# Five norms' running sums: tail tiles added on VectorE, fewer one-column sums on TensorE, root's table loaded earlier on ScalarE

## The reference

```python
def rmsnorm(x, g):
    return x * lax.rsqrt(jnp.mean(x * x, axis=-1, keepdims=True) + eps) * g
def _layer_norm(x, g, b):
    mu = jnp.mean(x, axis=-1, keepdims=True)
    var = jnp.mean(jnp.square(x - mu), axis=-1, keepdims=True)
    return (x - mu) * lax.rsqrt(var + LN_EPS) * g + b
# block 1
h = h + y @ w_out                                   # stage "out"
h = h + swiglu(rmsnorm(h, g_ffn), ...)              # "gu0", "down0"
h = rmsnorm(h, g_final)
# block 2, layer 0 and 1
x = _layer_norm(ALPHA * x + attention(x), ...)      # "out1", "out2"
x = _layer_norm(ALPHA * x + conv_ffn(x), ...)       # "gu1", "down1"; "gu2", "down2"
```

## Time and profile before

| | us |
|---|---|
| median of three runs | 1835.89 (1835.01 to 1836.67) |
| the profiled execution | 1835.84 |
| its span, first to last instruction | 1834.0 |
| TensorE busy | 1794.6 (98%) |
| GpSimd busy | 1034.7 (56%) |
| ScalarE busy | 783.4 (43%) |
| VectorE busy | 732.1 (40%) |

### The profile page before, as it was taken

The page is one execution under the profiler, slowest core; times in us unless marked ns, Lnnn a source line. Parts: engine busy times, 40 slices in busy tenths (PEclk is TensorE's granted clock), DMA queues, the critical chain, the costliest instruction groups (busy, mean ns, idle before and its releaser), DMA issues.

```text
span 1834.0 us, 26913 instructions
## 1 busy us (share of the span) xinstructions
PE 1794.6 (98%) x8816; PEld 1493.1 (81%) x8816; DVE 732.1 (40%) x1348; ACT 783.4 (43%) x1620; POOL 1034.7 (56%) x927
## 2 busy tenths in 40 slices
PE   8999999999999999999999999989999999999997
PEld 6879888888887888788888888878887888888886
DVE  7954000001125556453333322456765533333224
ACT  5434322332235556464444422545564644444221
POOL 6856665565562333466666654556554566656651
PEclk9999999999999999999999999999999999999999
DMA  5302333323334554323333232333332233332332
GB/s 150 92 23 82 104 102 98 96 77 109 88 86 113 133 127 114 97 66 109 92 102 91 84 106 86 81 81 87 91 79 57 78 103 100 94 99 82 103 90 96
DMA packets 327250, 171.92 MB, mean 94 GB/s; under 512 B 43458, under 2 KB 316948, under 8 KB 327188
## 3 DMA queue, kind: packets, MB, share of 16 engines
q1 hardware_dynamic: 327172, 171.12, 33.5%
q10 hardware_dynamic: 16, 0.00, 0.0%
HBM read 152.15 MB, written 2.10 MB: 84 GB/s over the span
## 4 chain that ended last, share of the span: by engine, by line
PE 83%; DVE 6%; ACT 4%; issue 2%; DMA 2%; SPq 1%; POOL 1%; ACTq 0%; DVEq 0%; POOLq 0%
PE bank L951 23%; PE bank L953 23%; PE bank L952 23%; PE attended L951 2%; PE attended L952 2%; PE attended L953 2%; DVE small L2324 1%; DMA raw<-in_a_w_in 1%; ACT pmap L1757 1%; PE turned L1348 1%; PE bank L1054 1%; PE bank L1042 1%; DVE PTL L2328 1%; ACT PTH L1762 1%; PE score L1332 0%
## 5 line engine op out<-in xcount | busy, mean ns | idle before, releaser
L720 POOL TENSOR_TENSOR WL<-raw,WH 128x512 fp32r<-128x512 f32 (+3 forms) x656 | 778.7, 1209 | 587.6 <-ACT WH L1514 586.9
L951 PE MATMUL bank<-XL,WH 128*128 128x512 f32 x1456 | 579.5, 398 | 7.1 <-DVE XL L2097 3.2
L953 PE MATMUL bank<-XH,WL 128*128 128x512 f32 x1456 | 567.9, 390 | 0.0
L952 PE MATMUL bank<-XH,WH 128*128 128x512 f32 x1456 | 567.7, 390 | 0.0
L1514 ACT ACTIVATE WH<-raw 128x512 fp32r<-128x512 f32 (+3 forms) x656 | 338.4, 566 | 306.3 <-PE bank L953 181.1
L951 PEld LDWEIGHTS bank<-XL,WH 128*128 128x128 f32 x1456 | 275.0, 189 | 62.3 <-DVE XL L2097 4.2
L953 PEld LDWEIGHTS bank<-XH,WL 128*128 128x128 f32 x1456 | 274.6, 189 | 58.2
L952 PEld LDWEIGHTS bank<-XH,WH 128*128 128x128 f32 x1456 | 275.1, 189 | 51.3
L951 PE MATMUL bank<-HL,WH 128*128 128x512 f32 (+1 forms) x528 | 200.6, 380 | 0.0
L952 PE MATMUL bank<-HH,WH 128*128 128x512 f32 (+1 forms) x528 | 200.3, 379 | 0.0
L953 PE MATMUL bank<-HH,WL 128*128 128x512 f32 (+1 forms) x528 | 200.3, 379 | 0.0
(11 more groups left out here) (322 smaller groups left out, 2474.4 us busy)
## 6 DMA issues: line engine op xcount, KB each, us to landing
raw<-in_ffn_w_in SPq DMA_DIRECT2D x88, 512.0 KB, 3.8
raw<-in_w_gate SPq DMA_DIRECT2D x22, 512.0 KB, 3.9
raw<-in_w_up SPq DMA_DIRECT2D x22, 512.0 KB, 3.8
raw<-in_ffn_w_out SPq DMA_DIRECT2D x28, 384.0 KB, 3.4
raw<-in_ffn_w_out SPq DMA_DIRECT2D x28, 320.0 KB, 3.2
raw<-in_a_w_in SPq DMA_DIRECT2D x16, 512.0 KB, 4.2
raw<-in_kv_w SPq DMA_DIRECT2D x32, 256.0 KB, 3.2
raw<-in_w_in SPq DMA_DIRECT2D x12, 512.0 KB, 3.9
```

The lines of the kernel that those rows point to most:

```text
L720: pool.tensor_tensor(wl, x, wh, ALU.subtract).then_inc(w_lo, 1)
L951: pe.matmul(out_, wh, xl, start=start, stop=False)
L952: pe.matmul(out_, wh, xh, start=False, stop=False)
L953: return pe.matmul(out_, wl, xh, start=False, stop=stop)
```

## The change

- **VectorE.** Behind `tail_out` of each half, new adds (`add_tail`) put each tail tile (layer norms only) and its squares into the running sums, 256 tokens at a time. Half 0: right behind each tail tile's residual add, values first and then the squares. Half 1: the values behind both residual adds, the squares behind pair 3. Behind out1 and out2 the sums stay in the PSUM banks until the last tail tile. The last add of squares raises the new counter `sum_full`.
- **TensorE.** `full_sums` takes the place of `whole_sums` and `half_stats` in the first five norms: 2 sums per half (RMS) or 4 (layer norm), behind a wait for `sum_full`. In half 0 it stands behind 5 of the 8 k of the first tail item (`SUMS_AT`), in the next stage behind k = 4; `half_widen` of half 1 moves from k = 5 to k = 6. In half 0 three k and one stand between sums and widening, where before it were four and one.
- **ScalarE.** `warm(ACT.Sqrt)` moves from behind the stage's last weight copy to the middle of the copies (out stages) or ahead of them (down stages), in all six places. The loop of `highs("out")` is written out.

```diff
+SUMS_AT = 5
@@ stage (out stages); the same in down
-                half_item(name, DT - 2, 0, hi, lo, 0, DT, 1, 0, 3)
-                whole_sums(m, 0)
-                half_item(name, DT - 2, 0, hi, lo, 0, DT, 1, 3, 4)
-                half_stats(m, 0)
-                half_item(name, DT - 2, 0, hi, lo, 0, DT, 1, 4).then_inc(item_done, 1)
+                half_item(name, DT - 2, 0, hi, lo, 0, DT, 1, 0, SUMS_AT)
+                full_sums(m, 0)
+                half_item(name, DT - 2, 0, hi, lo, 0, DT, 1, SUMS_AT).then_inc(item_done, 1)
@@ stage_in_halves
-                        if h == 0 and k == 2:
-                            whole_sums(m, 1)
-                        if h == 0 and k == 3:
-                            half_stats(m, 1)
-                        if h == 0 and k == 5:
+                        if h == 0 and k == 4:
+                            full_sums(m, 1)
+                        if h == 0 and k == 6:
                             half_widen(m, 1)
+            def full_sums(m, h):
+
+                pe.wait_ge(sum_full, 2 * (m - 1) + h + 1)
+                moments_of = ((0, ssq), (2, ssum)) if NORM[m] in CENTRED else ((0, ssq),)
+                for first, x in moments_of:
+                    for i, q in enumerate((2 * h, 2 * h + 1)):
+                        mm = pe.matmul(wide_rstd[h][:, first + i:first + i + 1], x[:, q * P:(q + 1) * P], ones[:, 0:1],
+                                       start=first == 0 and i == 0, stop=x is moments_of[-1][1] and i == 1)
+                mm.then_inc(stats_done, 1)
@@ ScalarE, highs_of_out; likewise in highs("out") at j == 4, and first in highs_of_down
                 for i in range(4, DT + 2):
+                    if i == 7:
+                        warm(ACT.Sqrt)
                     high(Nth(STAGES[name][0] + i))
@@ VectorE, norm_in_halves
+                in_banks = name in ("out1", "out2")
+
+                def add_tail(moment, h, i, x):
+                    c, last = slice(h * HALF, (h + 1) * HALF), i == len(tail) - 1
+                    total = (ssum, ssq)[moment][:, c]
+                    so_far = sum_banks[moment][:, c] if in_banks else total
+                    ins = dve.tensor_tensor(total if last else so_far, so_far, x, ALU.add)
+                    if last and moment:
+                        ins.then_inc(sum_full, 1)
+                    else:
+                        own.link(ins)
...
+                def add_squares_of(h, i):
+                    dve.wait_ge(half_squared, 2 * TAIL_BASE[name] + h * len(tail) + i + 1)
+                    add_tail(1, h, i, squares[i])
+
                 def tail_out(h):
...
+                        if h == 0:
+                            add_rows(h, i, t)
+                            add_squares_of(h, i)
+                    if h:
+                        for i, t in enumerate(tail):
+                            add_rows(h, i, t)
...
                 pair(0, 2)
                 pair(0, 3)
+                for i in range(len(tail)):
+                    add_squares_of(1, i)
                 moments(n, D, eps, 1)
```

More of the change, by code:

```diff
@@ L347, in two_blocks @@
         stats_done = sem("stats_done")
+        sum_full = sem("sum_full")
         var_ready = sem("var_ready")
@@ L1142, in down @@
                 part(3, 0).then_inc(half_done, 1)
-                part(2, 1, 0, 3)
-                whole_sums(m, 0)
-                part(2, 1, 3, 4)
-                half_stats(m, 0)
-                part(2, 1, 4).then_inc(item_done, 1)
+                part(2, 1, 0, SUMS_AT)
+                full_sums(m, 0)
+                part(2, 1, SUMS_AT).then_inc(item_done, 1)
                 part(3, 1, 0, WIDEN_AT)
@@ L1589, in highs @@
             def highs(name):
-                with act.Fori(0, 2) as it:
-                    for j in range(4):
-                        high(Nth(STAGES[name][0] + j + 2, it, 4))
+                for j in range(8):
+                    if j == 4:
+                        warm(ACT.Sqrt)
+                    high(Nth(STAGES[name][0] + j + 2))
             def highs_of_out(name):
@@ L1710, in _ @@
             highs("out")
-            warm(ACT.Sqrt)
             norm_in_halves(1, "gu0")
@@ L2020, in norm_in_halves, with add_rows @@
                 centred = n in CENTRED
+                in_banks = name in ("out1", "out2")
[8 more added lines that the diff above has]
+                        own.link(ins)
+                def add_rows(h, i, t):
+                    if not centred:
+                        return
+                    if h:
+                        dve.wait_ge(tail_read, TAIL_BASE[name] + i + 1)
+                    else:
+                        dve.wait_ge(bank_read[t % 2], (STAGES[name][1] + t) // 2 + 1)
+                    add_tail(0, h, i, xres[:, t, h * HALF:(h + 1) * HALF])
+                def add_squares_of(h, i):
+                    dve.wait_ge(half_squared, 2 * TAIL_BASE[name] + h * len(tail) + i + 1)
+                    add_tail(1, h, i, squares[i])
                 def tail_out(h):
                     c = slice(h * HALF, (h + 1) * HALF)
+                    dve.wait_ge(sum_tiles, SUM_BASE[name] + DT - len(tail))
                     for i, t in enumerate(tail):
@@ L2259, in add_up @@
                         dve.wait_ge(sum_tiles, SUM_BASE[name] + t)
-                        to = (ssum, ssq) if t == DT - 3 else (sum_banks[0][:, :], sum_banks[1][:, :])
+                        to = (sum_banks[0][:, :], sum_banks[1][:, :])
                         own.did(dve.tensor_tensor(to[0], sum_banks[0][:, :], xres[:, t, :], ALU.add))
```

5 lines of the change are left out of this document (removed).

## The result

The changed kernel takes 1842.88 us (1840.92 to 1845.30, 6 runs) against 1835.45 us (1833.25 to 1836.67, 6 runs) for the kernel before: ratio 1.0041, 95% interval 1.0031 to 1.0051. That is 6.7 us above the forecast of 1836.2, and above the range's end of 1840.0. The same kernel run again in the last series gave 1841.91 us, ratio 1.0025 (1.0016 to 1.0033). Both intervals lie above 1: it is slower, by 0.25 to 0.4%.

What follows compares the result with a forecast made beforehand. TensorE, busy 1794.6 of 1834.0 us, was held to bound the kernel except where norms feed it late. Terms out -0.1, down0 +0.7, out1 -1.7, down1 +2.5, out2 -1.0 gave +0.4: 1836.2 us, range 1830.0 to 1840.0.

Steps and rivals of the forecast that it cites:

- With 4 sums in a row I expect neither fall: Behind half 0's sums in out1 and out2 the clock would stay up, worth 1.3 us ahead of D each.
- D: The moment VectorE multiplies the first tile by half 0's widened root; forecast 2.97 us earlier in out1.
- Nobody waits: Half 0 of out1: adds and squares ready before TensorE reaches the sums, so no engine waits.
- 0.6 in out2: Half 0 of out2: TensorE waits 0.6 us at the sums, VectorE being blocked on tile 6's late square.
- Rival 5: Clock falls in new waits, half 1 of out1, down1 and out2: 1.7 us each, +5.5 in all, 1841.3 us; chance 10%.
- 1.3 us from D to the widening: Half 1 of out1, likewise out2: that stretch grows by 0.9 for row adds and 0.4 for small operations behind GpSimd.
- down1, right: Norm behind down1: adds take turns with GpSimd, TensorE waits 1.4 us; E shifts +0.7 + 0.5 + 1.3 = +2.5 us.
- E: The moment half 1's last half tile is split and TensorE can leave the two-item stage; its shift reaches the total.
- down0 and out: Norm behind down0: TensorE waits 0.8 us at half 0's sums, +0.7; behind out: no such wait, -0.1 us.
- rival 1: The new adds fall in GpSimd's pauses, so blocked terms go (out -0.9): -3.4 us, 1832.5 us; chance 11%.
- Rivals 2, 3 and 4: Half 1 costs nothing more, 1830.8, 14%; TensorE sets the end, 1821.4, 5%; GpSimd's queued XL go first, 1842.1, 10%.
- the mild half: The part of Rival 5 that lay inside the forecast range of 1830.0 to 1840.0 us.

Runs made afterwards that it cites:

- e2: The kernel before with the new sums in half 0 alone, half 1 and table loads as before: 1837.3 us, ratio 1.0009.
- e9: The changed kernel unaltered, measured and profiled a second time: 1841.9 us, ratio 1.0025 to the kernel before.
- e1: The kernel before with the new sums in half 1 alone, half 0 and table loads as before: 1842.2 us, ratio 1.0035.
- e10: The changed kernel with both residual adds and row adds of half 0 ahead of both square adds: 1839.0 us, ratio 1.0008.
- e4: The changed kernel with 16 extra products in TensorE's wait for XH4 behind each of out1, down1 and out2: 1837.0 us, ratio 1.0009.
- e5: The kernel of e1 with the same extra products as e4: 1841.5 us, ratio 1.0023.
- e11: The kernel of e6 with the row adds of half 1 behind pair 3, no longer ahead of pair 2: 1836.4 us, ratio 0.9998.
- e12: The kernel before with new sums only behind out, out1 and out2, half 0 ordered as in e6, out1 and out2's half 1 row adds late: 1831.8 us.
- e7: The kernel of e6 with the extra products of e4: 1836.1 us, ratio 0.9999.
- e6: The changed kernel with e10's order in half 0 and the table load of out1 and out2 ahead of their last six copies: 1839.3 us.

## Why the prediction was wrong, point by point

- **The step that failed: "With 4 sums in a row I expect neither fall".** It credited 1.3 us of clock in half 0 of out1 and again of out2. It took the sums for the whole cause. The changed kernel's 4 sums stand behind a wait of 1.18 to 1.59 us, and the clock fell in 4 of 4 (6 of 6 with e2); with a wait of 0.82 us at most it fell in 0 of 14. In out1 D comes 0.41 us earlier instead of 2.97: about the 1.7 us of sums less the 1.18 of wait, and nothing of the 1.3 of clock. In out2 it is 0.76 instead of 2.3, in e9 nothing in either. e1 and e2 say the same of the whole: half 1 alone cost 6.3 us against +5.5 in the sum, half 0 alone +1.4 against -5.1. The falls of 6.8 us in half 1, 1.7 us each from D to the widening in the first profile, come on top and are not in the second.
- **Half 0, "Nobody waits", and 0.6 in out2.** I set the square of tile 6 as ready in out1. I had seen VectorE blocked in order in out2 and priced it by one place of the last weight copy. The last copies begin anywhere from 2.16 us before the half to 0.18 behind its start in the 14 profiles, and were 0.36 and 0.18 before it here. Measured 1.18 and 1.45; e10 shows that the order was to blame. Against e10 the wait is 0.9 and 1.1 us longer, and D 2.2 and 1.3 us later: the rest is the clock. Even in the better order 0.20 to 0.46 us of wait stay in 11 of 12 cases.
- **Rival 5** named the mechanism, with a chance of 10%, for half 1 alone, and said that most of a fall would lie in waiting. A fall of 6.8 us, as in both out norms, outlasts the wait and slows the sums and the products up to the widening: 1.7 us of each were on the path, where it came. In e9's profiled execution it came in neither, and that one took 1842.8 us all the same, so this is not the step that the forecast broke on.
- **Half 1, right**: 1.3 us from D to the widening. e4 gives 1.30 and 1.29, e5 1.28 and 1.27; e9 1.33 in both; of it the row adds are 0.96 (e11) where the sum has 0.9.
- **down1, right with some luck**: +2.2 against +2.5. Measured from the norm's start D is 0.36 us later and not 0.7 (0.41 in e9), and D to E 1.8 longer, as in the sum (0.5 + 1.3). That the clock stayed up behind the wait there was luck, by the 5 of 8 above. The new adds, both inputs in SBUF, took 0.65 and 1.37 us beside GpSimd's two WL of 2.70, TensorE waited 0.98 and not 1.4, and in half 1 L1997 took 1.12 us instead of the 0.16 that it takes elsewhere, to the end of GpSimd's last XL:

```profile
1165.66 0.65 DVE L2032 TENSOR_TENSOR work<-work,xres 128x256 f32<-128x256 f32 x1
1166.35 1.37 DVE L2032 TENSOR_TENSOR work<-work 128x256 f32<-128x256 f32 x1
...
1164.74 2.70 POOL L722 TENSOR_TENSOR WL<-raw,WH 128x512 fp32r<-128x512 f32 x2 [1.93 <-ACT WH L1520]
...
1179.79 1.29 POOL L762 TENSOR_TENSOR XL<-xres,XH 128x512 fp32r<-128x512 f32 x1 [0.41 <-ACT XH L1573]
...
1179.99 1.12 DVE L1997 TENSOR_TENSOR small<-small 128x2 f32<-128x2 f32 x1
```

  The Trainium skill says in SBUF — State Buffer, Who interferes with whom, that a VectorE operation with two inputs in SBUF contends with a GpSimd operation that reads SBUF. The trace agrees, down to operations of two columns (1.12 us against 0.16).
- **down0 and out**: +0.4 against +0.7, with a wait of 0.35 us at the sums and not 0.8; -0.8 against -0.1. In out half 1's adds cost next to nothing (+0.1 us in e1), what rival 1 gave to that norm (-0.9).
- **Rivals 2, 3 and 4** fall: half 1 did cost 1.3, TensorE did not set the end (e12), and no add stood behind GpSimd's whole row (the longest took 1.37 us).
- **The range** took in only "the mild half" of rival 5. A mechanism whose size was known from the earlier trace rows, 1.7 us each, and that could strike in both halves of several norms deserved more than 10%. In half 0, where it struck each time, no rival had it.

## What to carry to other kernels

Work that leaves a nearly full TensorE is only a gain if no wait takes its place. In this kernel waits of 1.18 to 1.72 us ahead of a few short products went with a fall of the clock each time, those of 0.82 us and less never, and those about 1 us in five of eight; then the gain is lost twice, to the wait and to the clock. So order the feeding engine by when its inputs come (everything that is ready first, the operand from the slowest engine last), and make the change only in the halves where the removed work was on the path: here 24 of the 52 sums, in the better order, gave 6.6 us, and all 52 in the first order lost 5 to 7. And profile a kernel more than once before a row is called the cause: two profiles of the changed kernel gave +7.1 and +4.7 us over the same five norms.

## What the hardware showed that I had not expected

- 48 extra products went with a kernel 3.1 us faster (e7 against e6, same series), in e4_fill 2.9 to 5.9, part of which the fill can't have caused, and next to nothing in e5, where the clock fell 7 to 8 us further into the norm instead.
- Falls inside the norms are 3.4 or 6.8 us long, at a granted clock of 0.50 to 0.53 in the windows, and vary between executions of the same program: the changed kernel's mean clock was 0.986 to 0.990 in six executions, 0.988 to 0.992 in twelve others.
- The start of the last two weight copies relative to the half varied by over 2 us (2.16 us ahead of it to 0.18 behind) between kernels whose loads are the same. Their wait is for the load; why that lands late remains open.
